# Gate weights split by ScalarE and VectorE's steps interleaved in a one-core fp32 two-block kernel

## The reference

```python
mixed = jnp.concatenate([attn, conv_out], axis=-1) @ w_out[i]   # w_out 1024 x 1024
x = x + rms_norm(mixed, post_norm_gain[i])
e = rms_norm(p[i] @ w_ple_proj[i], ple_norm_gain[i])
x = x + jax.nn.sigmoid(x @ w_ple_gate[i]) * e
...
u, v, z = jnp.split(h @ w_in, 3, axis=-1)                       # h = rms_norm_2(x); w_in 1024 x 6144
```

## Time and profile before

| | |
|---|---|
| median of 3 runs | 887.78 us (886.39 to 889.26) |
| the profiled execution | 886.2 us, of which the span is 884.5 us |
| busy share | PE 98%, PEld 81%, DVE 65%, ACT 43%, POOL 58% |
| granted TensorE clock, mean | 0.995 of full speed |

### The profile page before, as it was taken

How to read it: one execution, slowest core, us unless ns; L and a number is a source line. 1 busy time by engine, 2 the same in 40 slices (tenths; PEclk the granted TensorE clock), 3 DMA queues, 4 the chain that set the end, 5 groups by cost and what they waited for, 6 DMA issues and landing times.

```text
span 884.5 us, 11934 instructions
## 1 busy us (share of the span) xinstructions
PE 866.4 (98%) x4196; PEld 720.4 (81%) x4196; DVE 574.9 (65%) x918; ACT 381.8 (43%) x826; POOL 516.5 (58%) x572
## 2 busy tenths in 40 slices
PE   8999999999998999999999999999998999999997
PEld 6888888888886787888888888888887888888876
DVE  6125648875996589765765535556996457888624
ACT  4123333433654277546112321112775536766622
POOL 7766556591249932217976038771359798566352
PEclk9999999999999999999999999999999999999999
DMA  7533221454952367895743262525962222112202
GB/s 198 167 120 96 73 92 51 143 119 88 233 179 72 121 145 165 212 215 190 159 127 96 67 195 90 127 94 145 221 182 72 72 72 91 53 48 72 72 1 95
DMA packets 83691, 106.84 MB, mean 121 GB/s; under 512 B 11953, under 2 KB 54449, under 8 KB 83634
## 3 DMA queue, kind: packets, MB, share of 16 engines
q1 hardware_dynamic: 72752, 85.12, 29.9%
q0 software_dynamic: 10880, 20.97, 14.0%
q10 hardware_dynamic: 2, 0.00, 0.0%
HBM read 103.98 MB, written 2.10 MB: 120 GB/s over the span
## 4 chain that ended last, share of the span: by engine, by line
PE 88%; POOL 5%; DVE 2%; ACT 2%; issue 1%; DMA 1%; DVEq 0%; POOLq 0%; ACTq 0%
PE bank L2173 26%; PE bank L2175 26%; PE bank L2174 26%; POOL wlo L873 2%; PE bank L2417 2%; PE bank L2445 1%; PE bank L2270 1%; POOL whi L864 1%; POOL rstd L821 1%; PE bank L2390 1%; POOL ms L818 1%; PE bank L2440 1%; PE bank L2439 1%; DMA raw<-in_a_w_in 1%; DVE wlo L1649 1%
## 5 line engine op out<-in xcount | busy, mean ns | idle before, releaser
L873 POOL TENSOR_TENSOR wlo<-raw,whi 128x512 fp32r<-128x512 f32 x184 | 252.6, 1404 | 0.7 <-ACT whi L999 0.7
L864 POOL TENSOR_SCALAR whi<-raw 128x512 fp32r<-128x512 f32 x182 | 130.7, 757 | 173.8 <-PE bank L2175 168.2
L2173 PE MATMUL bank<-actB_hi,whi 128*128 128x512 f32 (+1 forms) x416 | 159.5, 384 | 0.6 <-POOL wlo L873 0.6
L2174 PE MATMUL bank<-actB_lo,whi 128*128 128x512 f32 (+1 forms) x416 | 158.6, 381 | 0.0
L2175 PE MATMUL bank<-actB_hi,wlo 128*128 128x512 f32 (+1 forms) x416 | 158.5, 381 | 0.0
L2173 PE MATMUL bank<-whi,actA_hi 128*128 128x512 f32 x350 | 138.8, 396 | 5.3 <-POOL wlo L873 3.7
L2175 PE MATMUL bank<-whi,actA_lo 128*128 128x512 f32 x350 | 137.1, 392 | 0.0
L2174 PE MATMUL bank<-wlo,actA_hi 128*128 128x512 f32 x350 | 136.9, 391 | 0.0
L2173 PEld LDWEIGHTS bank<-actB_hi,whi 128*128 128x128 f32 x416 | 78.3, 188 | 15.3 <-issue 1.0
L2175 PEld LDWEIGHTS bank<-actB_hi,wlo 128*128 128x128 f32 x416 | 78.2, 188 | 15.2
L2174 PEld LDWEIGHTS bank<-actB_lo,whi 128*128 128x128 f32 x416 | 78.3, 188 | 14.2
(11 more groups left out here) (272 smaller groups left out, 1635.4 us busy)
## 6 DMA issues: line engine op xcount, KB each, us to landing
raw<-in_a_w_in SPq DMA_DIRECT2D x44, 512.0 KB, 4.0
raw<-in_w_in SPq DMA_DIRECT2D x32, 512.0 KB, 3.9
raw<-in_b_w_in SPq DMA_DIRECT2D x16, 512.0 KB, 3.4
raw<-in_a_w_out SPq DMA_DIRECT2D x12, 512.0 KB, 3.4
gain<-in_a_w_out POOLq DMA_DIRECT2D x9, 512.0 KB, 8.6
raw<-in_w_ple_gate SPq DMA_DIRECT2D x8, 512.0 KB, 4.3
gain<-in_a_w_in POOLq DMA_DIRECT2D x8, 512.0 KB, 7.4
raw<-in_a_w_in POOLq DMA_DIRECT2D x8, 512.0 KB, 7.7
```

Source lines behind the costliest of these rows:

```text
L864: pool.tensor_scalar(H, src[:, i * HALF:(i + 1) * HALF], 1.0, 1.0, ALU.mult, ALU.mult).then_inc(w_hi, 1)
L873: ins = pool.tensor_tensor(L, src[:, i * HALF:(i + 1) * HALF], H.bitcast(f32), ALU.subtract)
L2173: M(out_, whi_, xhi_, start=start, stop=False)
L2174: M(out_, whi_, xlo_, start=False, stop=False)
```

## The change

1. Gate unit 0's two upper halves are made by ScalarE (`hi_gate`) and not by POOL, after the second pair of `square_m1` and ahead of `ple_out(0)`. POOL's two roots for rows 2 and 3 of m1 move from between the two halves of gate 0 to behind them. VectorE's `post` for row 2 moves behind the `rest`s of row 0, and `post` for row 3 stands behind those of row 1 (before: behind both).
2. In the v4 products, ScalarE's `sum_hi` stands between the two weight halves of `hi_v4`, and no longer behind both.
3. In the sixth product of each group of seven (m == 5), VectorE's two lower weight halves stand between the combining steps, and no longer behind them.
4. The second lower half of `wo` 1 moves behind the last lower part of the convolution.

TensorE's and SyncE's lists are the same as before.

```diff
@@ split_half
-                for i in range(2 if n else 0):
+                for i in range(2 if n and (s, UNITS[u][1]) != ("gate", 0) else 0):
@@
-            after[at("gate", 0, 0)] = [lambda: root("m1", 2, D), lambda: root("m1", 3, D)]
-            after[at("gate", 0, 1)] = [mask_ws]
+            after[at("gate", 0, 1)] = [lambda: root("m1", 2, D), lambda: root("m1", 3, D), mask_ws]
@@ scalar
+            def hi_gate(n):
+                act.wait_ge(pe_block, last_block(SLOT_BEFORE[n]))
+                for h in range(2):
+                    src, landed, value = raw_of(n, h)
+                    act.wait_ge(landed, value)
+                    A(halves_of(n, 2 * h, 2)[0], src, ACT.Copy).then_inc(w_hi, 2)
@@
             for t in range(2):
                 square_m1(t, 1)
+            hi_gate(UNIT_NO["gate", 0])
             ple_out(0)
@@ for q in range(1, 14)
                 if 1 < q < 13:
-                    hi_v4(q + 1)
+                    hi_v4(q + 1, (0,))
                 if 2 <= q <= 4:
                     sum_hi(q - 1)
+                if 1 < q < 13:
+                    hi_v4(q + 1, (1,))
@@ vector
-                if i in (18, 20):
-                    lo_7("wo", (i - 18) // 2)
+                if i == 18:
+                    lo_7("wo", 0)
+                if i in (20, 21):
+                    lo_7("wo", 1, (i - 20,))
@@
-            for t in range(3):
+            for t in range(2):
                 post("m1", post_scaled, t, 1, x1_ready)
             for t in range(2):
                 for j in range(2):
                     rest("x1", t, j)
-            post("m1", post_scaled, 3, 1, x1_ready)
+                post("m1", post_scaled, 2 + t, 1, x1_ready)
@@ for q in range(1, 14)
                 if m == 5:
                     combine(g, 4, (2, 0), (2, 0), ALU.add, 0)
+                    lo_v4(q + 1, (0,))
                     combine(g, 2, (0, 1), (2, 0), ALU.subtract, 3)
+                    lo_v4(q + 1, (1,))
                     combine(g, 3, (2, 0), (2, 0), ALU.add, 3)
                 if 2 <= q <= 4:
                     act_sum(q - 1)
-                if 1 < q < 13:
+                if 1 < q < 13 and m != 5:
                     lo_v4(q + 1, (0,))
                 if 2 <= q <= 4:
                     act_sum_lo(q - 1)
-                if 1 < q < 13:
+                if 1 < q < 13 and m != 5:
                     lo_v4(q + 1, (1,))
```

## The result

The changed kernel takes 882.42 us (median of 4 runs, 881.81 to 882.54); the kernel before took 887.81 in the same comparison (4 runs, 886.39 to 889.26). The ratio is 0.9939, 95% interval 0.9923 to 0.9955: faster by 0.6%, more than the 0.3% that this measurement can tell. The forecast was 883.3 with a range of 880.6 to 886.6. The profiled execution took 882.5 us with a span of 880.8, against 886.2 and 884.5.

The account below looks back on a forecast made before the run. TensorE, busy 866.4 of 884.5 us, bounds the kernel. Gains 2.4 + 1.78 − 0.1 + 0.37 = 4.45 us take the profiled 886.2 to 881.75, or 883.3 against the median; range 880.6 to 886.6.

Parts of the forecast that it names:

- The stop at gate block 0: TensorE's 3.70 us wait for POOL's lower halves at 270.69, plus a slow-clock block after it, would go.
- Turns at the port: VectorE's two-SBUF-input instructions and POOL's alternate one for one beside the posts; POOL's four halves end at 263.5.
- The forecast's sum for the second half: At the gate, TensorE would wait 0.9 us for row 2's post and about 2.1 for row 3's.
- the term for part 1: Gate 0 and m1 row edits: 2.4 us gained of a possible 5.4.
- The second rival: At the gate, turns between VectorE and POOL cost nothing: all 5.4 us gained, 880.2 us; chance 0.1.
- the first rival: TensorE's clock falls again after idles of 0.9 and 2.1 us, costing 1.6: 884.9 us; chance 0.2.
- Parts 2 and 3: v4 products: stops ahead of blocks at 347.06, 352.88 and 358.78 go, gaining 0.94, 0.38 and 0.46, 1.78 us together.
- the transfers' rival: v4 products: late transfers, not order, hold them; the two product edits give only 0.3 us, 884.8 us; chance 0.1.
- The 0.1 that was charged for it: v4 products: 0.1 us deducted for later transfer landings, with 0.15 us of slack at the half ending at 387.29.
- Part 4: Second product of w_out, near 220.51: the stop goes as the convolution's lower part stands between the halves, 0.37 us.
- Gate 2's slack: POOL's gate 2 halves: slack shrinks from 1.6 to about 0.7 us, costing nothing, or up to 0.6 of stall.
- The order of the posts: VectorE at the gate: post 2 behind row 0's rests ends at 270.7, post 3 behind row 1's at 276.4.

Follow-up runs that it names:

- p1_gate: Kernel before with only the gate 0 edits (ScalarE upper halves, roots behind POOL's lower halves, posts among the rests): 883.84 us, ratio 0.9963.
- writes_only: Changed kernel plus eleven write-only IOTA instructions on POOL between the mask and gate 1's halves: 887.16 us, ratio 1.0000 to the kernel before.
- gates_by_two: gate0_by_two with gate 1 also split by ScalarE and VectorE, not POOL: 879.02 us, ratio 0.9910 to the kernel before.
- p2_sum: Kernel before with only ScalarE's upper part of a sum put between the two weight halves: 885.93 us, ratio 0.9986.
- gate0_by_two: Changed kernel with gate 0's lower halves made by VectorE, POOL's roots and mask ahead: 879.87 us, ratio 0.9921 to the kernel before.
- p23_v4: Kernel before with only the two v4 product reorderings (ScalarE's sum, VectorE's lower halves): 885.05 us, ratio 0.9969.
- after_again: Changed kernel, unchanged, run again: 881.23 us, ratio 0.9935 to the kernel before.
- all_old_posts: Changed kernel with row 2's post put back ahead of row 0's rests: 881.65 us, ratio 0.9937 to the kernel before.

## Why the prediction was right, point by point

- **The stop at gate block 0** (3.70 us and a clock at 0.57) is gone, as written. p1_gate shows that part 1 does it alone.
- **Turns at the port.** Forecast: four lower halves of some 1.8 us, ending at 263.5, and post 1 at 265.4. Measured: 1.73 each, 262.65 and 265.14. The forecast's sum for the second half was a little long: the stops of 0.61 and 1.70 us idle cost 0.8 and 1.9 where 0.9 and 2.1 stood. And the old stop with its fallen clock had cost 5.5 and not 5.4 (gate block 0 could have begun at 265.96 + 0.79 = 266.75, 3.94 before it did, and took 1.58 too long). So the term for part 1 is 2.79 and not 2.4. writes_only and gates_by_two show the mechanism itself: without POOL instructions that read from SBUF the same post takes 2.7 us and not 4.4. The Trainium skill (SBUF — State Buffer, section "SBUF: two separate sides") says that VectorE with two SBUF inputs is held up only by a GpSimd operation that reads SBUF; the IOTA rows agree, with 1.40 us for post 3's pair beside them.
- **The second rival** (no turns, 880.2; its own terms give 880.3) is excluded by the two stops.
- **The clock did not fall again** with idles of 0.61 and 1.70 us, so the first rival did not come. The 1.6 us that the fall costs came from one execution. Without it, two gate blocks and the transposes between take 6.45 us; five of the six profiles with the stop show 7.78 to 8.06, so the fall costs 1.3 to 1.6. The sixth is p2_sum. There the granted clock is 0.50 in 270 to 274 and 0.68 in 274 to 278, and from the first matmul of gate block 0 to the transposes of row 3 it took 9.30 us, against 278.72 − 270.69 = 8.03 in the earlier trace rows. The fall costs 1.3 us more there. A cost that varies like this could be part of why the medians differ by 5.4 us and the two profiled spans by 3.7, and so of the 0.9 us by which the changed kernel's median is below the forecast: its executions spread over 0.7 us, those of the kernel before over 2.9. This is not shown: gate0_by_two has no fall at the gate either and spread over 2.7, and most of the difference stays open.
- **Parts 2 and 3**: 1.68 forecast, 1.72 by TensorE's rows, and no stop where the transfers' rival wanted one. p23_v4 shows that this rival is not empty: two stops of 0.23 and 0.45 us idle in an execution in which transfers landed later. The 0.1 that was charged for it lies between nothing and 1.2 (0.23 + 0.45, twice 0.16 and twice 0.1 for the slower first step).
- **Part 4**: 0.37 forecast, 0.48 by the rows. The 0.1 is the first matmul's slower step (0.31 for 0.23), which the working charged at the gate and left out here.
- **Gate 2's slack**: 0.7 forecast; its lower halves end at 294.18 and the block starts at 295.70, so 1.5 is left. writes_only shows what happens when it is used up.
- **What no step named**: 0.98 us given back by the transposes near 665. ScalarE's L1373 is waited for there; the two transfers of the value weights, issued at 638.5, landed 6.4 us later where it took 4.8 before, and POOL's and VectorE's steps behind them came later. after_again has 1.93 us of idle there, gate0_by_two 1.72, all_old_posts 1.47, the kernels without the whole change 1.48 to 1.73. Over all thirteen profiles the idle follows these two transfers: 1.47 to 1.51 where they took at most 5.4 us, 1.59 at 5.5, 1.72 and 1.73 at 5.8, then 1.93, 2.07 and 2.39 at 6.0, 6.1 and 6.4. It differs between executions of one kernel (2.39 and 1.93), and four of the five profiles that arrive there 4 us or more earlier have more idle than 1.49. Whether an earlier arrival makes these transfers slower was not tested and stays open.
- **The order of the posts**, on which the working spent several steps, is worth nothing in time here (all_old_posts), because the two orders meet two limits of nearly equal length. The working was right on where TensorE waits with the new order. It did not ask what the old one would give.

In the sum, 2.79 + 1.72 + 0.48 − 0.98 = 4.0 us against 4.45 forecast for the profiled execution. With the 0.37 by which this execution began behind, that is the 3.7 between the spans. The three parts gave 4.99 together, 0.5 more than forecast, and the loss that no step named took nearly twice that back. The forecast's 883.3 for the median is 0.9 above 882.42, while its 881.75 for the profiled execution is 0.8 below 882.54. That both are so near is in part luck: errors of opposite sign cancel.

## What to carry to other kernels

When VectorE is the engine that others wait for, count what POOL reads from SBUF beside it: each such instruction is put into VectorE's line, and moving it to ScalarE, or even to VectorE itself, can be faster than leaving it on an engine that seems free. Ask of an order of deliveries not only which wait it removes but which limit comes next: here both orders of the posts cost TensorE the same to 0.03 us, one by waiting for the last delivery, the other by its own work behind a late first one. What did shorten the line was work taken out of it, or out of what it takes turns with. And follow a delay on a queue to the last thing behind it, not to the next one: the changed kernel has 4.9 us of slack at gate 1 (ready at 278.02, wanted at 282.94) and 1.5 at gate 2, and writes_only lost its time at the second.

## What the runs showed of the hardware

- VectorE's and POOL's reading instructions alternate one for one: four lower halves and VectorE's two short ones went at 1.73 and 1.75 us each, where alone they take 1.27 (2.54 for two in gates_by_two's profile) and 0.70 (1.40 for two). A long add beside two halves took 2.20 for 1.23.
- POOL's small instructions are held too: in the changed kernel's trace the 128x1 `ms` instruction (L818) took 1.37 to 1.39 us beside VectorE's 1024-wide instruction with two SBUF inputs, and 0.30 alone.
- IOTA, which reads nothing, was not held up and did not hold up: eleven in 5.63 us beside posts 2 and 3, each between 0.544 and 0.552 us, and post 3's pair at 1.40 beside them.
- The granted clock fell behind a stop of 3.70 us in all six profiles that have it and behind the one of 5.38, and in none of the profiles behind 2.51 or behind 0.61 and 1.70. Near 665 it fell in some executions (the kernel before, with 1.49 us of idle; after_again, 1.93; gates_by_two, 2.07) and not in others (the changed kernel's first profile, 2.39), so the length of the last idle alone does not tell. The fall at the gate cost 1.3 to 1.6 us in five profiles and 2.85 in one; the fall near 665 cost nothing, since TensorE waits for ScalarE there.
